# Hybrid decoder layer: spare buffers for the last sequence's V pages, a second queue for the first q and k chunk, and one explicit load of the gelu set

## What is computed

```python
# stick-breaking attention; each of the 8 sample tokens has 64 pages of 128 past keys and values
z = einsum('bqhd,bkhd->bhqk', q, k) * HEAD_DIM ** -0.5 + bias
log_keep = where(mask, log_sigmoid(-z), 0.0)
later = cumsum(log_keep, axis=3, reverse=True) - log_keep
w = where(mask, exp(log_sigmoid(z) + later), 0.0)
att = einsum('bhqk,bkhd->bqhd', w, v)
...
# feed-forward, D_FF = 2816, three taps over time on the gate branch
gate, up = xn @ w_gate, xn @ w_up
conv = conv_b + sum(padded[:, i:i + t] * conv_w[i] for i in range(3))
x = x + rmsnorm((gelu(conv) * up) @ w_down, g_post_ffn)
```

## Time and profile before

| | |
|---|---|
| median of 3 runs | 3632.18 us (3630.4 to 3633.06) |
| profiled execution: its own time | 3639.77 us |
| its span in the profile | 3638.1 us |
| mean granted TensorE clock | 0.95 |
| busy: PE, DVE, ACT, POOL | 92%, 56%, 39%, 18% of the span |
| attention | from about 671 to 1737 us |
| feed-forward | from about 2069 to 3638 us |

### The profile page before, as it was taken

One profiled execution on the slowest core, in us unless ns is written; L12 is line 12 of the kernel. 1 busy time (PEld: TensorE's weight loads), 2 busy tenths in 40 slices (PEclk: granted clock), 3 DMA queues, 4 the chain that ended last, 5 costly groups with the idle time before them and its releaser, 6 DMA issues. The chain is left out here.

```text
span 3638.1 us, 48630 instructions
## 1 busy us (share of the span) xinstructions
PE 3346.9 (92%) x14901; PEld 2305.5 (63%) x14901; DVE 2042.9 (56%) x2832; ACT 1401.6 (39%) x2214; POOL 637.5 (18%) x725
## 2 busy tenths in 40 slices
PE   6999875699999999998699799999999999999998
PEld 5888652343444444343588587787778777877777
DVE  5110449799888988985445455425542555245542
ACT  4110110365665666563333344324432443223332
POOL 2000054354444443442011100000000000000000
PEclk8999977799999999998799899999999999999999
DMA  3211261579889888986445433433343334334333
GB/s 128 76 65 56 82 79 28 165 255 300 283 289 304 276 287 284 302 295 221 157 139 154 129 98 93 134 110 104 93 133 110 105 93 124 123 124 121 122 108 116
DMA packets 487628, 569.61 MB, mean 157 GB/s; under 512 B 64808, under 2 KB 308616, under 8 KB 485321
## 3 DMA queue, kind: packets, MB, share of 16 engines
q1 hardware_dynamic: 482950, 549.81, 49.0%
q10 hardware_dynamic: 4328, 17.05, 1.2%
q0 software_dynamic: 176, 0.56, 0.0%
HBM read 506.91 MB, written 59.30 MB: 156 GB/s over the span
## 5 line engine op out<-in xcount | busy, mean ns | idle before, releaser
L2273 PE MATMUL ffn_bank<-ffn_xh,ffn_wh 128*128 128x512 f32 x1408 | 557.8, 396 | 19.0 <-DVE ffn_wl L2487 18.6
L2273 PE MATMUL ffn_bank<-ffn_xl,ffn_wh 128*128 128x512 f32 x1408 | 549.4, 390 | 0.0
L2273 PE MATMUL ffn_bank<-ffn_xh,ffn_wl 128*128 128x512 f32 x1408 | 548.8, 390 | 0.0
L1291 POOL TENSOR_TENSOR att_S<-att_S,att_X 128x512 f32<-128x512 f32 (+3 forms) x256 | 345.5, 1349 | 291.9 <-PE att_bank L1574 231.9
L1474 DVE TENSOR_TENSOR att_prod<-att_Kr,att_q_wide 128x1024 f32<-128x1024 f32 x256 | 324.5, 1268 | 13.0 <-DMA att_Kr<-in_cache_k_dram 9.5
L1569 PE MATMUL att_bank<-att_X,att_negtri 128*128 128x512 f32 (+3 forms) x640 | 299.7, 550 | 30.7 <-DVE att_X L1445 30.2
L2273 PEld LDWEIGHTS ffn_bank<-ffn_xh,ffn_wh 128*128 128x128 f32 x1408 | 264.9, 188 | 95.1 <-DVE ffn_wl L2487 31.4
L1479 DVE TENSOR_REDUCE att_z_s<-att_prod 128x16 f32<-128x1024 f32 x256 | 313.2, 1223 | 8.8
L2273 PEld LDWEIGHTS ffn_bank<-ffn_xh,ffn_wl 128*128 128x128 f32 x1408 | 264.9, 188 | 56.3
L2273 PEld LDWEIGHTS ffn_bank<-ffn_xl,ffn_wh 128*128 128x128 f32 x1408 | 265.2, 188 | 52.6
L2491 DVE TENSOR_TENSOR ffn_wdl<-ffn_wdf,ffn_wdh 128x1024 fp32r<-128x1024 f32 x88 | 107.5, 1225 | 334.8 <-ACT ffn_wdh L2397 334.7
(11 more groups left out here) (378 smaller groups left out, 5930.3 us busy)
## 6 DMA issues: line engine op xcount, KB each, us to landing
att_Kr<-in_cache_k_dram SPq DMA_DIRECT2D x512, 256.0 KB, 3.8
att_Vr<-in_cache_v_dram SPq DMA_DIRECT2D x512, 256.0 KB, 3.8
ffn_wdf<-in_w_down_dram SPq DMA_DIRECT2D x108, 512.0 KB, 3.3
ffn_stage<-in_w_gate_dram SPq DMA_DIRECT2D x89, 512.0 KB, 3.9
ffn_stage<-in_w_up_dram SPq DMA_DIRECT2D x88, 512.0 KB, 4.5
qku_work<-in_x_prompt_dram SPq DMA_DIRECT2D x16, 512.0 KB
att_qf<-qT_dram SPq DMA_DIRECT2D x64, 128.0 KB, 3.7
att_kf<-kT_dram SPq DMA_DIRECT2D x64, 128.0 KB, 3.7
```

The lines of the kernel that those rows point to most:

```text
L1291: pool.tensor_tensor(new[:, r:], old[:, r:], x[:, r:], ALU.add).then_inc(s_part, 1)
L2273: mm = pe.matmul(bank[:, first + f % 2, :], w[:, j, k, :], x[:, k, :], start=(k == 0 and n == 0), stop=(k == KD - 1 and n == 2))
```

## The change

Attention: the last sequence's V pairs 16 to 23 go into the eight slots of `Kr` as these come free in the last round, and pairs 24 to 27 into the buffers `qf` and `kf`, each with its own semaphore (`spare_loaded`, 12 of them). Pairs 28 to 31 go on using `Vr`. PE reads these pages from there. The first chunk of q and k of head 0 is loaded by four DMAs from ACT's queue, behind ACT's table load, instead of from SP's. Feed-forward: ACT loads table set 11 once, ahead of its first split.

```diff
+SPARE = KSLOTS + 4
...
+        def start_qk(eng, b, c):
+            i = NCH - 1 - c
+            for x, src in ((qf, "qT"), (kf, "kT")):
+                for half in range(2):
+                    eng.dma_start(x[half * HD:(half + 1) * HD, i, :], A[src][bass.ds(b * HD, HD), c * CH:(c + 1) * CH]
+                                  ).then_inc(qk_loaded[i], 16)
+
+        def spare_page(n, k):
+
+            i = n - VSLOTS
+            if i < KSLOTS:
+                return Kr[:, i, k, :]
+            return (qf, kf)[(i - KSLOTS) // 2][:, 2 * (i % 2) + k, :]
...
+                def load_v_spare(row, n, free):
+                    load_pages("cache_v", lambda k: spare_page(n, k), spare_loaded[n - VSLOTS], row, n, free)
+
+                for c in reversed(range(NCH - 1)):
                     load_qk(0, c)
...
                         elif not last:
                             load_k(row_next, n + KSLOTS - NKK, k_free)
+                        else:
+                            load_v_spare(row, VSLOTS + n + KSLOTS - NKK, k_free)
...
-                for n in range(VSLOTS, NKK):
+                for n in range(VSLOTS + KSLOTS, VSLOTS + SPARE):
+                    load_v_spare(row, n, (qk_lo, H * 2 * NCH))
+                for n in range(VSLOTS + SPARE, NKK):
                     load_v(row, n, (v_used, (H - 1) * NKK + n - VSLOTS + 1))
...
             def _(act):
                 act.add_instruction(mybir.InstLoadActFuncSet(name=nc.get_next_instruction_name(),
                                                              act_func_set_id=EXP_LN_SET, ins=[], outs=[]))
+                start_qk(act, 0, NCH - 1)
...
+                    spare = last_seq and VSLOTS <= n < VSLOTS + SPARE
                     for i in (n - 1, n):
-                        pe.wait_ge(v_loaded[i % VSLOTS], 16 * PP * (b * (NKK // VSLOTS) + i // VSLOTS + 1))
+                        if spare:
+                            pe.wait_ge(spare_loaded[i - VSLOTS], 16 * PP)
+                        else:
+                            pe.wait_ge(v_loaded[i % VSLOTS], 16 * PP * (b * (NKK // VSLOTS) + i // VSLOTS + 1))
...
+                act.add_instruction(mybir.InstLoadActFuncSet(name=nc.get_next_instruction_name(),
+                                                             act_func_set_id=GELU_SET, ins=[], outs=[]))
                 split(0, 0)
                 for k in range(KD):
                     split_x(0, k)
```

More of the change, by code:

```diff
@@ L43 @@
 EXP_LN_SET = 6
+GELU_SET = 11
 class Stage:
@@ L1123, in stage_attention @@
         k_loaded, v_loaded = m.sems("k_loaded", KSLOTS), m.sems("v_loaded", VSLOTS)
+        spare_loaded = m.sems("spare_loaded", SPARE)
         k_used, k_summed, v_used = m.sem("k_used"), m.sem("k_summed"), m.sem("v_used")
@@ L1179, in load_qk @@
                         sp.nop().then_inc(waited, 1)
[L1180 to L1183, removed]
+                    start_qk(sp, b, c)
                 def load_v_head(b, c):
@@ L1191, in load_v_head, with load_pages @@
                     sp.dma_start(vh[:, 4 * c:4 * c + 4, :], v[:, 4 * c:4 * c + 4, bass.ds(b * HD, HD)]).then_inc(v_piece[c], 16)
-                def load_pages(which, ring, sem, row, n, free):
+                def load_pages(which, place, sem, row, n, free):
                     low = NPG - (n + 1) * PP
@@ L1202, in load_pages @@
                     for k, page in enumerate(pages):
-                        sp.dma_start(ring[:, k, :], cache[which][bass.ds(page, 1)].rearrange("o s c -> s (o c)")).then_inc(sem, 16)
+                        sp.dma_start(place(k), cache[which][bass.ds(page, 1)].rearrange("o s c -> s (o c)")).then_inc(sem, 16)
                 def load_k(row, n, free=None):
-                    load_pages("cache_k", Kr[:, n % KSLOTS], k_loaded[n % KSLOTS], row, n, free)
+                    load_pages("cache_k", lambda k: Kr[:, n % KSLOTS, k, :], k_loaded[n % KSLOTS], row, n, free)
                 def load_v(row, n, free=None):
-                    load_pages("cache_v", Vr[:, n % VSLOTS], v_loaded[n % VSLOTS], row, n, free)
-                for c in reversed(range(NCH)):
+                    load_pages("cache_v", lambda k: Vr[:, n % VSLOTS, k, :], v_loaded[n % VSLOTS], row, n, free)
+                def load_v_spare(row, n, free):
+                    load_pages("cache_v", lambda k: spare_page(n, k), spare_loaded[n - VSLOTS], row, n, free)
+                for c in reversed(range(NCH - 1)):
                     load_qk(0, c)
@@ L1511, in _, with samples_v @@
                 pe.wait_ge(consts, 8)
-                def samples_v(b, n):
+                def samples_v(b, n, last_seq=False):
                     if n % 2 == 0:
@@ L1524, in samples_v @@
                             g = (i % 2) * PP + k
-                            mm = pe.matmul(bank[g * QUAD:g * QUAD + H, S_B, :], w_s[:, :, i * PP + k], Vr[:, i % VSLOTS, k, :],
+                            page = spare_page(i, k) if spare else Vr[:, i % VSLOTS, k, :]
+                            mm = pe.matmul(bank[g * QUAD:g * QUAD + H, S_B, :], w_s[:, :, i * PP + k], page,
                                            start=(n == 1), stop=(n == NKK - 1), skip_group_check=True)
@@ L1609, in _ @@
                 for n in range(NKK):
-                    samples_v(NS - 1, n)
+                    samples_v(NS - 1, n, True)
                 finish_sequence(NS - 1)
```

## The result

The changed kernel takes 3597.99 us (median of 4, 3596.02 to 3599.57) against 3631.38 us for the kernel before (4 runs, 3630.4 to 3633.06). The ratio is 0.9906, with a 95% interval of 0.9892 to 0.992: 33.4 us faster, with 29 to 39 as the interval. The forecast was 3592.0 with a gain of 40.2. So the direction is right and the size about 7 us too good. The two profiled executions differ by exactly 40.2 (3639.77 and 3599.57), and that is chance: 6.3 us of it lie ahead of attention, where nothing was changed (the executions in this document need from 662.7 to 672.1 us up to there, whatever the edit).

What follows compares the result with a forecast made beforehand. PE is busy for 92% of the span, so a change pays only where PE stands still or runs at half clock. 23.2 + 14.5 + 2.5 = 40.2 us, off 3632.18, gives 3592.0 us; range 3587 to 3601.

Steps and rivals of the forecast that it cites:

- feed-forward: Looped feed-forward tiles: without the table loads 27 iterations gain 0.86 us each, 23.2 us; bounds 14.6 to 27.1.
- V pages: Value phase of attention's last sequence: spare buffers end it at 1716.70 instead of 1731.16, 14.5 us; bounds 11.4 to 18.2.
- first chunk: Start of attention: four q/k DMAs issued by ACT instead of SP gain 2.5 us; bounds 1.5 to 2.8.
- rounds: Attention's rounds: nothing counted; about 3 us, a step of delay, if the spare pages delay the last K pages.
- Nothing takes its place: Feed-forward iteration: without the load `wl` ends 0.64 us before PE wants it, so no other wait replaces the stall.
- the free load at the head: Feed-forward's head: the added load's 1.28 us fit into ACT's 12.85 us idle before its first work; cost 0.
- the free gelu load: Feed-forward, ahead of the gelu: this load lies where ACT waits for DVE's taps; no gain counted separately.
- the first iterations of blocks 1 and 2: Feed-forward: their waits, 1.63 and 1.7 us, stay because DVE still adds the previous block's result; nothing counted.
- The rival that the table loads stay: Feed-forward loop heads still get their loads despite the explicit one; only 17.0 us gained, 3615.2 us; chance 0.06.
- The half-returned stall: Feed-forward: PE still waits a little, only the named idle of 14.6 us returns; 31.6 in all, 3600.6 us; chance 0.08.
- the last group runs at half clock: End of the last sequence's value phase: behind a 2.4 us standstill PE's last group takes 1.91 us.
- without the first four everything behind moves by 2.50: Start of attention, SP's queue: K pages issued at 683.47 instead of 685.97, DVE's first product at 686.92 instead of 689.42.

Runs made afterwards that it cites:

- load_at_gate: The changed kernel with one gelu-set load put back in each of the 30 looped iterations, ahead of the gate copy; 3620.78 us, one run.
- late_pad: The changed kernel with 96 empty ACT instructions ahead of attention, and ACT issuing the first q/k chunk only after the page row landed; 3584.8 us, one run.
- best: The changed kernel with 96 empty instructions, page row ahead of the chunk, and `prod` as spare for V pairs 28 and 29; 3583.44 us, ratio 0.9875.
- spare_only: The kernel before with only the last sequence's V pages in K slots and q/k buffers; 3615.23 us, ratio 0.9954.
- pad_past: The changed kernel with 96 empty ACT instructions in the stage ahead of attention; 3592.0 us, ratio 0.989.
- pad_short: The changed kernel with 40 empty ACT instructions in the stage ahead of attention; 3594.24 us, one run.
- load_at_gelu: The changed kernel with one gelu-set load put back in each of the 30 looped iterations, ahead of the gelu; 3599.89 us, one run.
- after: The changed kernel itself, against the kernel before; 3597.99 us, ratio 0.9906.
- pad_front: The kernel before with five empty instructions in ACT's queue in place of the four DMA issues, no DMA moved; 3645.46 us, ratio 1.003.

## Why the prediction was right, and what it missed

With the executions side by side each term has several measurements. The means are of the executions that have the part against those that don't:

| term | forecast | measured |
|---|---|---|
| feed-forward | 23.2 | 1566.1 (5) - 1540.5 (8) = 25.6 |
| V pages | 14.5 | 32.97 (5) - 17.87 (7) = 15.1 |
| first chunk | 2.5 | 18.56 (5) - 17.60 (7) = 1.0 |
| rounds | 0 | 1008.5 (4) - 1016.6 (5) = -8.1 |
| sum | 40.2 | 33.6 (33.4 by the medians) |

(feed-forward leaves load_at_gate out; value leaves out the two with `prod`; start leaves out late_pad and best; rounds: kernels with 80 or 81 packets and no part of the queue, against those with the jump at 870.)

**Feed-forward: right, and slightly small.** The loop loss was 0.86 an iteration; 22.62 - 21.77 = 0.85 came back. "Nothing takes its place" held, and so did the free load at the head and the free gelu load. I had counted nothing for the first iterations of blocks 1 and 2, and their waits fell too, from 1.63 and 1.7 to 1.2 at most: 0.9 together. 27 x 0.85 + 0.9 = 23.9; that leaves 1.7. Most of these lie behind the last iteration of block 2, where the kernel before has no load: from there to the end of the span the five executions without the part take 583.1 us in the mean and six with it 581.7, and both kinds vary between 580.4 and 584.4. So this remainder is no effect of the loads that these runs can show.

**The rival that the table loads stay** fell at once: line 2454 has none. The half-returned stall fell as well, since PE's waits for `wl` are three and the cadence gave back more than the idle time that the profile names.

**V pages: right, with one price wrong.** The issue was forecast 6.57 behind PE's start and came 1706.25 - 1699.85 = 6.40 behind. The last group came 15.49 behind the start (1715.34), forecast 15.98. What was off is the step "the last group runs at half clock": it took 1.20 and not 1.91. The granted clock was 1.00 up to 1716 and 0.52 from there to 1720, so it did fall, but as the group ended; the sum over heads behind it ran at half clock (1.87 for what takes 1.05 in best). The other executions fall on both sides: the last group took 1.06 in spare_only, pad_past, pad_short and load_at_gate, behind waits of 1.67 to 2.42, and 1.85 and 1.91 in load_at_gelu and late_pad, behind waits of 2.17 and 1.56. The forecast price came true in two of seven, and the length of the wait doesn't tell which; what does stays open. The spare pages cost the round before nothing, though the DMA engines went to 0.97.

**First chunk: the mechanism was there, its size wrong.** The step that failed is "without the first four everything behind moves by 2.50". It took SP's queue as the only thing in the row. But between the page row's copy and SP's next issue lies the landing of that small DMA, and with ACT's 512 KB on the same DMA engines it landed 3.24 us behind its issue instead of 1.8. That gives back 1.4 of the 2.5. The prediction looked for competition only among the q and k chunks. It also had ACT issue behind its table load, at 672.12 in the time of the earlier trace rows, where ACT issues at once (664.58, beside the load); but even by its own time ACT's first DMAs stood ahead of the page row's copy, which SP issues at 672.87. late_pad shows the cause by taking it away: 1.78 us again. The part then gives 2.0 in the start (18.56 - 16.57). The Trainium skill, "DMA: Bandwidth & Descriptors", section "Issuing engines are not separate DMA queues", which the prediction weighed as 0.4 us, has the rule that they interleave on the same 16 engines; it costs more here than by the bytes moved, because SP's queue waits for the small DMA.

**The rounds: missed wholly.** The prediction costed what the four new issues do, and not where they push the instructions behind them. That is not a price that was mis-sized but an effect without a term, since nothing outside the three places was counted: with the loop four instructions further on ACT stands still for 2.7 to 4.5 us at each of the five jumps of after while instructions are fetched, and the rounds take 8 us longer. pad_front shows this without any of the change's DMAs, pad_past takes it away and comes out at 3592.0 us. That this is the number of the forecast is partly luck: the feed-forward term was 2.4 small, the V pages 0.6 small, and the chunk's 1.5 large. That the changed kernel's own time, 3597.99, lies in the stated range is luck as well: the upper end, 3601, was set for the half-returned stall and not for this.

## What to carry to other kernels

Price an instruction on a busy engine by what waits for it, not by its duration: a load of 1283 ns cost 0.85 us in one place of the iteration and nothing two instructions further on. When an edit adds or takes away instructions ahead of a long loop, look at the gap at the loop's jump and at the packet count of the instruction queues; a loop that has become slower as a whole, with no operation in it changed, may only have been shifted, and some empty instructions tell that in one run. Ahead of bulk DMAs from a second queue, let the small one go first that the other queue waits for.

## What the runs showed of the hardware

- **The place of a loop in an engine's program has a price.** A loop of some 336 instructions that lies four further on in ACT's program made eight rounds 8 us longer, and the kernel 0.3% slower (pad_front, 1.003 [1.0017, 1.0044]). ACT stood still at each of five jumps, 4.50 us and 2.92 at two of them in after, 2.45 and 3.58 in pad_front; the queue q14 had 105 packets and not 81, and at the jump shown above four of them start within the standstill.
- **An engine's queue issues DMAs beside its own table load.** ACT's first DMA was issued at 664.58, the load ran from 664.55 to 665.83.
- **A table load takes 1283 ns and the next activation follows at once.** In load_at_gate the load at 2123.23 ends at 2124.51, and the gate copy behind it starts at 2124.52. The Trainium skill, "ScalarE: Activation LUTs", section "What ACT_TABLE_LOAD costs", adds some 1380 ns of drain for a switch to another set. This load is not a switch. In the kernel before it is one, from set 11 to set 0, and the load at 2112.43 is followed by its gate copy at 2113.72 as well: no drain shows there either.
